# Hybrid diffusion step on one core: expert rows at fixed places, routing done tile by tile between the output products, and expert weights requested before routing

## The chip, the cores and the metric

The kernel runs on 1 core of a Trainium2 chip, in float32 throughout. The metric is the device time of one execution in microseconds (us). The kernel before takes 1537.15 us, the median of 3 runs (1534.24 to 1538.37).

## The reference

Two trunk layers over 128 context (prompt) tokens and 512 latent tokens, model width 1024. Layer 0 mixes tokens by multi-head latent attention, layer 1 by grouped-query attention; both are followed by a mixture of experts. Every sub-layer has RMS normalisation, a shift and scale, and a gate on its result; shift, scale and gate come from the conditioning vectors by one 1024 x 6144 linear map per layer (the modulation). Cut to the part around the change:

```python
for l in range(DEPTH):                                   # 2 layers
    mod_p = (silu(c_ctx) @ ada_w[l] + ada_b[l])[None]    # 6 vectors of 1024: shift, scale, gate (attention), the same (experts)
    mod_s = silu(c) @ ada_w[l] + ada_b[l]
    ...                                                  # attention; its output product is w_o (1024 x 1024)
    xp = xp + gt_a_p * mix_p;  xs = xs + gt_a_s * mix_s
    hp = modulate(rms_norm(xp, norm_ffn[l]), sh_m_p, sc_m_p);  hs = ...
    xp = xp + gt_m_p * hier_moe(hp, ...);  xs = xs + gt_m_s * hier_moe(hs, ...)

def hier_moe(h, ...):                                    # 640 tokens, 4 groups of 4 experts
    g_prob = softmax(xt @ w_group + b_group);  g_w, g_idx = top_k(g_prob, 1)
    e_in = (xt @ w_exp + b_exp)[the 4 experts of group g_idx]
    e_val, e_idx = top_k(e_in, 2);  e_w = softmax(e_val) * g_w
    out = sum over the 2 experts of e_w * (silu(xt @ w_gate) * (xt @ w_up)) @ w_down    # 1024 x 256, 256 x 1024
```

The outputs are the normalised tokens of both groups and the keys and values of the context tokens.

## The kernel before

Tokens lie in five tiles of 128 rows (tile 0 the prompt, 1 to 4 the latents). Each engine has one program, written out in order; engines hand over by semaphores. SP (SyncE) issues the weight loads in one fixed order; ScalarE's queue issues small loads and stores; POOL (GpSimd) issues the zeroing and the indexed scatters and gathers.

**Stages.** (1) Modulation products of layer 0's first columns, `ada(j)`, L1199: each takes a 1024 x 384 piece of `ada_w` (1.57 MB), on four column groups of TensorE; ScalarE copies the result out and stores it (`mod_out`, L498), and `mod_fetch` (L511) loads the pieces back for VectorE's `modulation` (L788). There are 32 such products: 6 ahead of the projection (`ADA_START`), 16 in the heads of layer 0 (two per head pair, hooks at steps 2 and 9 of ten), 10 in the heads of layer 1. (2) The projection of layer 0, tile by tile (`projection`, L1341), VectorE and ScalarE working on the result of tile t (`post_m`, L916; L684 to L694) before TensorE may start tile t + 1. (3) The heads (`heads`): eight head pairs of ten steps, each step scores, maximum, exponential, scaling, transposes and value product. (4) The mixes: `mix(l, it)`, L1238, the attention output product of one tile, 16 products of 128 x 512 (two records each). VectorE adds the result to the residual (L842) and makes the normalised, modulated tile `h` (L1107 to L1114). TensorE transposes it (`turn_h`), ScalarE copies it out, and `logits(t)` (L1430) multiplies it by the 20 router columns, two tiles behind the mixes. (5) When all five tiles have logits, `routing(l)` (L1004) picks group and experts for all tiles at once, TensorE ranks the rows of each expert (L1453 to L1455), and VectorE works out for every token and choice a row in the table `slot_rows`, for each of 25 possible tiles its expert, and how many tiles are needed. Only then POOL scatters: ten indexed DMAs of 128 rows (L461). (6) SP waits for `routed`, requests gate and up weights of the first two tiles and the down weights of the first (L367 to L371), waits for all scatters, and loads the rows of the first three tiles (L360). Expert rows are packed: an expert's rows begin at the tile behind the last of the expert before. (7) The expert loop: for each tile, rows in, transpose (L1465), gate and up (L1473), down (L1490), rows back to the table (L637). 17 tiles ran in layer 0 and 19 in layer 1. Weights lie in a ring of four slots (L284 to L293), which also serves `w_o`, `w_uq` and layer 1's q, k, v weights. (8) Gathers (L472), weighting, residual.

The table (25 x 128 rows of 1024) is zeroed by POOL from the end of layer 0's projection on (L453 to L455), 25 DMAs of 512 KB. At step 6 of the last head pair (L583 to L594) ScalarE's queue requests six broadcast rows (two of them the attention gates, `gate_a`) and the router's weights. The modulation of layer 1's first columns (`mod_fetch(1, 0)`, L615; `modulation(1, 0)`, L1117; `turn_mods(1)`, L1457) stands behind the routing of layer 0.

## Time and profile before

| | |
|---|---|
| median of 3 runs | 1537.15 us |
| profiled execution | 1533.43 us, its span 1531.6 us |
| mean granted TensorE clock | 0.905 of 2.4 GHz |
| TensorE busy | 1252.3 us (82%) |
| VectorE, ScalarE, POOL busy | 538.3, 408.0, 62.0 us |
| HBM read, written | 229.48 MB, 45.96 MB |

The page of the profile gives the span in 40 slices of 38.3 us; each digit is a busy share in tenths, and PEclk the granted clock in tenths:

```profile
PE   3487999999989609999929994999989609999980
PEclk8698999999999759999969996999989759999995
DMA  9904822333410097999982005430110087999955
```

Slices 0 to 3 are loads and the projection of layer 0, 4 to 11 its heads, 12 and 13 the mixes and routing, 14 to 19 the experts; 20 to 29 are layer 1's projection and heads, 30 to 33 mixes and routing, 33 to 38 the experts. A low PE digit with a low clock digit is a place where TensorE waits.

### The profile page before, as it was taken

The numbers are of one execution on the slowest core, as the hardware profiler recorded it, in microseconds if no ns is written. First come the engines' busy times: TensorE is split into PE (matmuls) and PEld (weight loads), VectorE is DVE, ScalarE is ACT, GpSimd is POOL, SyncE is SP. The second block draws the span as 40 slices with busy tenths as digits, with TensorE's granted clock in tenths as the row PEclk, the third lists the DMA queues.
The fourth block names the chain that finished last, engine by engine and source line by source line (L and its number), as shares of the span: only waits on it lengthen the run. The fifth ranks groups of instructions, "written<-read, shape, count | busy, mean of one in ns | idle before, by whom it ended". The sixth has DMA issues, their size and how long they took to land.

```text
span 1531.6 us, 16577 instructions
## 1 busy us (share of the span) xinstructions
PE 1252.3 (82%) x5784; PEld 687.5 (45%) x5784; DVE 538.3 (35%) x1115; ACT 408.0 (27%) x807; POOL 62.0 (4%) x70
## 2 busy tenths in 40 slices
PE   3487999999989609999929994999989609999980
PEld 0254566666645404444414542555545404444430
DVE  0231444445523311111136454566623311111116
ACT  2022344444421100111122225666621100111113
POOL 0003200000000020000020000000000020000002
PEclk8698999999999759999969996999989759999995
DMA  9904822333410097999982005430110087999955
GB/s 342 358 4 109 267 93 92 117 97 118 138 45 0 13 325 252 361 373 370 312 299 96 0 1 179 136 133 32 38 48 1 26 303 252 371 364 363 377 206 205
DMA packets 161284, 276.32 MB, mean 180 GB/s; under 512 B 12017, under 2 KB 122820, under 8 KB 160836
## 3 DMA queue, kind: packets, MB, share of 16 engines
q1 hardware_dynamic: 135440, 207.77, 39.1%
q0 software_dynamic: 9360, 34.08, 6.7%
q10 hardware_dynamic: 16420, 33.62, 6.1%
q8 instruction: 40, 0.66, 0.2%
q14 instruction: 24, 0.20, 0.0%
HBM read 229.48 MB, written 45.96 MB: 180 GB/s over the span
## 4 chain that ended last, share of the span: by engine, by line
PE 77%; DVE 7%; DMA 5%; SPq 3%; ACT 3%; issue 2%; ACTq 1%; DVEq 1%; POOL 1%; POOLq 0%
PE ps L1473 16%; PE ps L1235 10%; PE ps L1194 9%; PE ps L1253 9%; PE ps L1490 8%; PE ps L1284 6%; PE ps L1406 5%; PE ps L1373 3%; PE ps L1527 3%; PE ps L1209 2%; PE ps L1366 1%; PE ps L1383 1%; DMA arena<-slot_rows 1%; DVEq L784 1%; PE ps L1433 1%
## 5 line engine op out<-in xcount | busy, mean ns | idle before, releaser
L1194 PE MATMUL ps<-const,arena 128*128 128x128 f32 (+2 forms) x1290 | 200.1, 288 | 141.9 <-DMA arena<-slot_rows 68.6
L1194 PEld LDWEIGHTS ps<-const,arena 128*128 128x128 f32 (+2 forms) x1290 | 156.8, 147 | 233.3 <-issue 69.5
L1473 PE MATMUL ps<-arena 128*128 128x512 f32 x576 | 257.4, 600 | 4.4 <-DVE arena L1121 4.4
L869 DVE TENSOR_REDUCE hst<-ps 128x1 f32<-128x640 f32 (+1 forms) x160 | 114.5, 716 | 151.9 <-PE ps L1406 88.5
L1473 PEld LDWEIGHTS ps<-arena 128*128 128x128 f32 x576 | 108.0, 193 | 128.7 <-issue 125.2
L1235 PE MATMUL ps<-arena 128*128 128x512 f32 (+2 forms) x400 | 154.8, 547 | 9.9 <-DVE arena L840 6.6
L557 ACT ACTIVATE arena<-ps 128x640 f32<-128x640 f32 (+1 forms) x160 | 99.0, 619 | 195.8 <-PE ps L1194 177.9
L1121 DVE COPY arena<-ps 128x1024 f32<-128x1024 f32 x36 | 44.1, 1224 | 301.0 <-PE ps L1194 300.9
L1253 PE MATMUL ps<-arena 128*128 128x512 f32 x320 | 138.8, 593 | 1.8 <-issue 1.8
L1490 PE MATMUL ps<-arena 128*128 128x512 f32 x288 | 129.7, 593 | 1.9 <-DVE arena L1130 1.9
L562 ACT ACTIVATE arena<-ps,hst 128x640 f32<-128x640 f32 (+1 forms) x160 | 112.6, 704 | 17.5 <-DVE hst L869 17.5
L1235 PEld LDWEIGHTS ps<-arena 128*128 128x128 f32 x400 | 77.6, 196 | 82.8 <-issue 70.1
L1284 PE MATMUL ps<-arena 128*64 128x128 f32 x1344 | 106.6, 287 | 0.4 <-ACT arena L557 0.4
L1406 PE MATMUL ps<-arena 128*128 128x320 f32 (+1 forms) x288 | 93.3, 442 | 1.4 <-issue 1.4
L1253 PEld LDWEIGHTS ps<-arena 128*128 128x128 f32 x320 | 60.2, 190 | 74.9 <-issue 74.9
L1284 PEld LDWEIGHTS ps<-arena 128*64 128x64 f32 x1344 | 71.8, 138 | 48.0 <-issue 42.6
L627 ACT ACTIVATE arena<-ps 128x256 f32<-128x256 f32 x36 | 13.8, 384 | 295.3 <-PE ps L1473 295.3
L877 DVE TENSOR_SCALAR arena<-arena,hinv 128x640 f32<-128x640 f32 (+1 forms) x160 | 80.7, 504 | 12.8 <-issue 0.4
L1490 PEld LDWEIGHTS ps<-arena 128*128 128x128 f32 x288 | 52.1, 190 | 54.9 <-issue 52.6
L634 ACT ACTIVATE arena<-ps 128x1024 f32<-128x1024 f32 x36 | 36.8, 1023 | 140.9 <-PE ps L1490 140.9
L1209 PE MATMUL ps<-arena,cond 128*2 128x384 f32 x512 | 53.6, 541 | 19.8 <-DMA arena<-in_ada_w 13.4
L1527 PE MATMUL ps<-arena 64*128 64x320 f32 (+1 forms) x288 | 61.5, 478 | 6.6 <-ACT arena L739 4.8
(141 smaller groups left out, 874.6 us busy)
## 6 DMA issues: line engine op xcount, KB each, us to landing
arena<-in_ada_w SPq DMA_DIRECT2D x64, 768.0 KB, 6.3
arena<-in_moe_w_gate SPq DMA_DIRECT2D x36, 1024.0 KB, 7.1
arena<-in_moe_w_up SPq DMA_DIRECT2D x36, 1024.0 KB, 9.7
arena<-in_moe_w_down SPq DMA_DIRECT2D x72, 512.0 KB, 9.1
arena<-slot_rows SPq DMA_DIRECT2D x36, 512.0 KB, 10.6
slot_rows<-arena ACTq DMA_DIRECT2D x36, 512.0 KB, 7.1
slot_rows<-arena POOLq DMA_DIRECT2D x25, 512.0 KB, 12.2
arena<-mod_rows ACTq DMA_DIRECT2D x16, 512.0 KB, 6.2
```

Of the source, the lines that this page charges most:

```text
L557: act.activation(ptbuf(l, j, keys), ps[:, 4 * BANK:4 * BANK + keys], ACT.Copy).then_inc(S("pt_ready"), 1)
L562: act.activation(split(pbuf(l, s, keys), 2 if keys > P else 1), scores(s, keys), ACT.Exp, bias=hst[:, b:b + 1], accum_out=hsum[:, b:b + 1] ...
L869: nc.vector.tensor_reduce(hst[:, b:b + 1], scores(s, step(s)[3]), AX.XY, ALU.max, negate=True)\
L1194: return nc.tensor.transpose(out, in_, ident[0:rows, 0:rows])
L1209: last = mm(ada_bank(j)[ADA_Q * g:ADA_Q * g + 2, :], c[:, k], w[:, k], start=r == 0, stop=r == KD // ADA_G - 1)
L1235: last = mm(bank(2 + b, cols), hT[l](t)[:, k * P:(k + 1) * P], w[:, k], start=k == 0, stop=k == KD - 1)
L1253: last = mm(bank(mix_bank(it) + half), oT_block(l, k, it), w[:, k], start=k == 0, stop=k == KD - 1)
L1284: last = mm(oT_out(it)[VD * odd:VD * (odd + 1)], v_of(2 * m + odd, first + j), ptbuf(l, 2 * p + odd, blocks * P)[:, j * P:(j + 1) * P], st ...
L1406: last = mm(scores(s, keys)[:, c], m_qT[:, at:at + P], m_kT[:, k:k + w], start=True, stop=True)
L1473: last = mm(bank(2 + u % 2), e_xsT[:, (u % 2) * D + k * P:(u % 2) * D + (k + 1) * P], w[:, k], start=k == 0, stop=k == KD - 1)
L1490: last = mm(bank(6 + n), e_hidT[:, (u % 2) * FF + k * P:(u % 2) * FF + (k + 1) * P], w[:, k, n * BANK:(n + 1) * BANK], start=k == 0, stop= ...
L1527: last = mm(scores(s, keys)[:, c], g_qT[half, q:q + P], g_kT[half, at:at + w], start=True, stop=True)
```

## The change

- **Fixed rows.** Expert e has rows 640 e to 640 e + 639 of the table, whatever the others get; the first 16 tiles are the first 128 rows of experts 0 to 15, and only tiles beyond an expert's first are worked out (`OVER` = 9 of them). The table has 10,368 rows (a spare tile at the end) and is zeroed in 11 DMAs. Rows are read and written by an address read from `first_row`.
- **Routing tile by tile.** `pick` and `place_rows` do for one tile what `routing` did for five, two tiles behind the mixes; POOL scatters a tile's two copies when `slotted` says so. What is left of `routing` is the numbering of the overflow tiles and the weights; it stands behind the copy of the first transposed rows.
- **Router on column groups.** The router's 20 columns, padded to 32, are the stationary operand, on four column groups; ScalarE copies the 128 x 128 result out and a matmul with a selection matrix sums the groups and transposes back. The mix is cut into four parts, with router pieces between them.
- **Early weights.** Gate and up weights of experts 0 and 1 are requested before the mixes (layer 0) or in the heads (layer 1), down 0 and gate and up 2 when the mixes end. The ring starts two slots further.
- **Modulation.** Ten products move from layer 1's heads into layer 0's projection, two per tile; the other 16 of the layer 0 heads are now all of layer 1. `mod_fetch`, `mod_store` and `modulation(l, 1)` move from head pair 5 to head pair 0. `gate_a` is fetched behind the heads. Layer 1's first columns are turned behind the second mix of layer 0.

```diff
@@ SP: the loads
         def experts(l):
-            R = rounds_needed(sp, l)
-            e, e1 = expert_of(0), expert_of(1)
-            load_gu(l, 0, e)
-            load_gu(l, 1, e1)
-            load_dn(l, 0, e)
+            load_gu(l, 0, 0)
+            load_gu(l, 1, 1)
+            sp.wait_ge(S("mixed"), NTILE * (l + 1))
+            load_dn(l, 0, 0)
+            load_gu(l, 2, 2)
             sp.wait_ge(S("rows_scattered", l), 16 * 2 * NTILE)
             load_rows(l, 0, 0)
             load_rows(l, 1, 1)
+            sp.wait_ge(S("gu_done", l), 1)
+            load_dn(l, 1, 1)
             load_rows(l, 2, 0, 1)
+            load_rows(l, 3, 1, 2)
+            R = rounds_needed(sp, l)
...
         load(S("dkv_landed"), w_dkv, A["mla_w_dkv"][0], KV)
+        sp.wait_ge(S("mod_landed"), 64)
+        for j in range(ADA_START, ADA_START + 4):
+            load_ada(j)
         load(S("uk_landed"), w_uk, A["mla_w_uk"], D)
         load(S("uv_landed"), w_uv, A["mla_w_uv"], D)
-        sp.wait_ge(S("ada_made"), 4)
+        for j in range(ADA_START + 4, ADA_N - 2):
+            load_ada(j)
         load(S("uq_landed"), w_uq, A["mla_w_uq"], HEADS * P)
+        for j in range(ADA_N - 2, ADA_N):
+            load_ada(j)
         load(S("wo_landed", 0), w_wo0, A["mla_w_o"][0], BANK, 0)
-        for j in range(ADA_START, ADA_START + 2 * PAIR):
+        for j in range(ADA_N, 2 * ADA_N):
             load_ada(j)
         sp.wait_ge(S("made"), len(MAKES) * PAIR)
         load(S("wo_landed", 0), w_wo1, A["mla_w_o"][0], BANK, BANK)
+        sp.wait_ge(S("ada_made"), 2 * ADA_N)
         R = experts(0)
@@ POOL
-        for t in range(SLOT_TILES):
-            pool.dma_start(split_rows(slots[t * P:(t + 1) * P, :]), bmid(zeros, KD)).then_inc(S("table_zeroed"), 16)
+        for a in range(0, ROWS, KD * P):
+            b = min(a + KD * P, ROWS)
+            n = (b - a) // P
+            pool.dma_start(slots[a:b, :].rearrange("(p r) n -> p r n", r=n), bmid(zeros, n)).then_inc(S("table_zeroed"), 16)
         for l in range(2):
-            pool.wait_ge(S("routed", l), 1)
             for t in range(NTILE):
+                pool.wait_ge(S("slotted", l), t + 1)
                 for c in range(2):
                     pool.indirect_dma_start(
...
@@ ScalarE
         def experts(l):
+            act.wait_ge(S("pv_done"), NTILE * PAIR * (l + 1))
+            for v in range(2):
+                rows_in(gate_a[:, v * D:(v + 1) * D], l, 2, v, S("gates_a", l))
+            if l == 0:
+                mod_fetch(1, 0)
+            for t in range(NTILE + 2):
+                if 2 <= t:
+                    parts_out(t - 2)
+                if 1 <= t <= NTILE:
+                    hT_out(t - 1)
...
@@ VectorE
+        def pick(l, t):
+            lg, o, m = rt(T_LG, NR), rt(T_O, NR), rt(T_M, G5)
+            dve.wait_ge(S("logits", l), t + 1)
+            op(nc.vector.tensor_tensor(lg, bank(2, NR, P), rbias[:, l * NR:(l + 1) * NR], ALU.add)).then_inc(S("logits_in", l), 1)
+            first_max(o, lg, m, rt(T_MX, G5), rt(T_SC, NR), G5)
+            ...
+            op(nc.vector.tensor_tensor(M, m12[:, 0:NE], m12[:, NE:], ALU.add)).then_inc(S("picked", l), 1)
+            ...
+        def place_rows(l, t):
+            dve.wait_ge(S("ranked", l), t + 1)
+            op(nc.vector.tensor_tensor(tb, bank(3, NE, t * NE), const[:, C_EB:C_EB + NE], ALU.add))
+            op(nc.vector.tensor_tensor(split(t2, 2), split(m12, 2), bmid(tb, 2), ALU.mult))
+            op(nc.vector.tensor_reduce(pl, split(t2, 2), AX.X, ALU.add))
+            op(nc.vector.tensor_copy(slot_i[:, 2 * t:2 * t + 2], pl)).then_inc(S("slotted", l), 1)
...
             for t in range(NTILE):
+                if t >= 2:
+                    pick(l, t - 2)
                 residual(l, t)
+                if t >= 2:
+                    place_rows(l, t - 2)
                 row_stats(f"ffn{l}", t, t + 1, t)
                 ...
-            routing(l)
-            if l == 0:
-                modulation(1, 0)
+                if l == 0 and t == 1:
+                    modulation(1, 0)
+            pick(l, NTILE - 2)
+            place_rows(l, NTILE - 2)
+            pick(l, NTILE - 1).then_inc(S("shifted", l), 1)
+            place_rows(l, NTILE - 1)
             xsT(0, 0)
+            routing(l)
             hid(0, 0)
@@ TensorE
                 project(l, t, parts, out_sem)
+                if l == 0:
+                    for j in ada_between(t):
+                        ada(j)
...
+            for t in range(NTILE):
+                mix(l, t, 0)
+                if t >= 2:
+                    logits_part(t - 2)
+                mix(l, t, 1)
+                if t >= 2:
+                    logits(t - 2)
+                mix(l, t, 2)
+                mix(l, t, 3)
+                if t >= 2:
+                    rank(t - 2)
+                if t >= 1:
+                    turn_h(t - 1)
+                if l == 0 and t == 1:
+                    turn_mods(1)
+            logits_part(NTILE - 2)
+            logits(NTILE - 2)
+            turn_h(NTILE - 1)
+            logits_part(NTILE - 1)
+            logits(NTILE - 1)
+            rank(NTILE - 2)
+            rank(NTILE - 1)
```

`logits_part(t)` is 8 products with the router's 32 columns stationary and 128 token columns moving; `logits(t)` is the one with the selection matrix; `rank(t)` is one product for tile 0, two for tiles 1 to 3 and four for tile 4. VectorE's copy of the latents in step 4 of the last head pair of layer 0 waits for `table_zeroed`, since the zeros lie where that copy goes.

## Rows read from the trace of the kernel before

**Rows 1.** Stages by window: us, busy PE, PEld, DVE, ACT, POOL, PEclk, DMA share, GB/s.

```profile
77.00:90.00 13.00, 10.81 (x46) 7.58 (x46) 5.38 (x20) 3.00 (x11) 0.00 (x0) 1.00 0.03 11
526.00:577.00 51.00, 3.89 (x16) 3.13 (x16) 13.25 (x71) 1.51 (x2) 9.71 (x10) 0.50 0.71 254
600.00:766.00 166.00, 166.00 (x494) 80.93 (x493) 28.14 (x43) 20.73 (x29) 0.00 (x0) 1.00 1.01 356
```

**Rows 2.** The chain of waits, layer 0, mix to experts: start us, us, what.

```profile
497.69 13.73 PE ps L1253 x32
553.20 11.96 DMA slot_rows<-arena,slot_i
565.18 9.14 DMA arena<-slot_rows
577.65 8.83 PE ps L1473 x16
600.40 6.87 PE ps L1473 x16
```

**Rows 3.** The chain of waits, layer 1, the same stretch.

```profile
1187.18 13.73 PE ps L1253 x32
1266.18 9.30 PE ps L1473 x16
```

**Rows 4.** Timeline, layer 0: start us, us, engine line op out<-in [idle before <-releaser].

```profile
519.46 1.97 PE L1194 MATMUL ps<-const,arena 128*128 128x128 f32 x8 [1.68 <-DVE arena L1114]
528.83 0.17 DVE L1038 TENSOR_REDUCE arena<-arena 128x5 f32<-128x20 f32 x1 [0.28 <-issue]
531.60 0.17 DVE L1053 TENSOR_TENSOR arena<-arena 128x5 f32<-128x5 f32 x1
541.71 1.03 POOL L461 DMA_INDIRECT slot_rows<-arena,slot_i  x1 [364.15 <-DVE expert L1094]
541.87 1.01 DVE L798 TENSOR_REDUCE modt<-arena 32x128 f32<-32x512 f32 x1 [0.21 <-issue]
543.32 0.34 DVE L802 SCALAR_TENSOR_TENSOR modt<-modt,mod_vec 32x128 f32<-32x128 f32 x1
```

**Rows 5.** DMA to landing by source line: L360, then L461, then L472.

```profile
DMA to landing us min/median/max: 3.2/10.6/12.6
DMA to landing us min/median/max: 3.8/10.1/12.0
DMA to landing us min/median/max: 4.4/6.3/10.3
```

**Rows 6.** Chain after layer 0's second mix; VectorE's timeline there.

```profile
464.99 13.73 PE ps L1253 x32
469.92 1.23 DVE L1114 TENSOR_TENSOR arena<-arena 128x1024 f32<-128x1024 f32 x1
```

**Rows 7.** The chain of waits in the heads of layer 1.

```profile
1013.21 1.41 PE ps L1209 x16
1035.28 1.41 PE ps L1209 x16
1080.32 0.82 DVE hst L869
1099.58 0.82 DVE hst L869
```

**Rows 8.** Timeline at the end of those heads: ScalarE's queue, then TensorE.

```profile
1108.33 4.80 ACTq L593 DMA_DIRECT2D rw<-in_moe_w_expert  x1
1114.08 1.30 PE L1194 MATMUL ps<-const,arena 128*128 128x128 f32 x5 [6.55 <-ACT arena L557]
```

**Rows 9.** Layer 0: the chain before its projection; TensorE's timeline in it.

```profile
49.63 8.05 DMA mod_vec<-in_vec_m
90.09 9.28 PE L1235 MATMUL ps<-arena 128*128 128x384 f32 x32 [1.90 <-DVE arena L840]
```

**Rows 10.** DMA queue of POOL from 135 to 192 us: packets, MB, share.

```profile
q0 software_dynamic: 3596, 13.11, 80.9%
```

More of the change, by code:

```diff
@@ L1061, in routing @@
-            nc.vector.tensor_tensor(before[:, 0:NE], M1[:, 0:NE], M2[:, 0:NE], ALU.add)
-            for t in range(1, T5):
-                settle()
-                last = nc.vector.tensor_tensor(before[:, t * NE:(t + 1) * NE], before[:, (t - 1) * NE:t * NE],
-                                               M[:, t * NE:(t + 1) * NE], ALU.add)
-            last.then_inc(S("picked", l), 1)
-            dve.wait_ge(S("ranked", l), 1)
-            op(nc.vector.tensor_tensor(split(over, NE), blast(bank(3, NE, T5 * NE), T5), bmid(const[:, C_OV:C_OV + T5], NE), ALU.is_gt))
+            over, nt, cs, c2 = new(LAT * NE), new(NE), new(NE), new(NE)
@@ L1070, in routing @@
+            excl, av = new(NE), new(NE)
+            ge1, ge2 = new(OVER * NE), new(OVER * NE)
+            te, row, dummy = new(OVER), new(OVER), new(OVER)
+            need, rnd, den = new(ROUNDS), new(1), new(T5)
+            assert n[0] <= 1024, n[0]
+            op(nc.vector.tensor_tensor(split(over, NE), blast(bank(3, NE, T5 * NE), LAT), bmid(const[:, C_OV + 1:C_OV + T5], NE), ALU.is_gt))
             op(nc.vector.tensor_reduce(nt, split(over, NE), AX.X, ALU.add))
@@ L1092, in routing @@
+            op(nc.vector.tensor_tensor(dummy, dummy, const[:, C_DUM:C_DUM + OVER], ALU.mult))
+            nc.vector.tensor_scalar(te, te, float(NE - 1), None, ALU.min)
+            op(nc.vector.tensor_tensor(row, row, dummy, ALU.add))
+            nc.vector.tensor_copy(first_row[:, 0:NE], const[:, C_EB:C_EB + NE])
+            nc.vector.tensor_copy(first_row[:, NE:], row)
+            nc.vector.tensor_copy(expert[:, 0:NE], const[:, C_TI:C_TI + NE])
             nc.vector.tensor_copy(rounds[:, 0:1], rnd)
@@ L1247, in mix @@
                 pe.wait_ge(S("pt_ready"), (l + 1) * STEPS)
-            if it >= 2:
+            if it >= 2 and part == 0:
                 pe.wait_ge(S("mix_out"), l * NTILE + it - 1)
-            for half in range(2):
-                w = split(halves[half], KD)
-                for k in range(KD):
-                    last = mm(bank(mix_bank(it) + half), oT_block(l, k, it), w[:, k], start=k == 0, stop=k == KD - 1)
-            last.then_inc(S("mixed"), 1)
+            half, ks = part // 2, range(KD // 2 * (part % 2), KD // 2 * (part % 2 + 1))
+            w = split((w_wo0, w_wo1)[half], KD)
+            for k in ks:
+                last = mm(bank(mix_bank(it) + half), oT_block(l, k, it), w[:, k], start=k == 0, stop=k == KD - 1)
+            if part == 3:
+                last.then_inc(S("mixed"), 1)
         def spare_free(l, m, r):
@@ L1428, in turn_h @@
                 last.then_inc(S("h_turned", l), 1)
-            def logits(t):
-                pe.wait_ge(S("hT_out", l), t + 1)
-                for k in range(KD):
-                    last = mm(bank(2, NR, t * 32), e_hT[:, (t % 2) * D + k * P:(t % 2) * D + (k + 1) * P], rw[:, k * NR:(k + 1) * NR],
-                              start=k == 0, stop=k == KD - 1)
-                last.then_inc(S("logits", l), 1)
-            mix(l, 0)
-            mix(l, 1)
-            turn_h(0)
-            pe.wait_ge(S("router_landed", l), 32)
@@ L1441, in experts, with logits_part @@
-            for t in range(2, NTILE):
-                mix(l, t)
-                logits(t - 2)
-                turn_h(t - 1)
+            def logits_part(t):
+                pe.wait_ge(S("hT_out", l), t + 1)
+                if t:
+                    pe.wait_ge(S("logits_in", l), t)
+                for r in range(KD // ADA_G):
+                    for g in range(ADA_G):
+                        k = ADA_G * r + g
+                        last = mm(bank(2, P)[RWC * g:RWC * (g + 1)], rw[:, k * RWC:(k + 1) * RWC],
+                                  e_hT[:, (t % 2) * D + k * P:(t % 2) * D + (k + 1) * P], start=r == 0, stop=r == KD // ADA_G - 1)
+                last.then_inc(S("logits_part", l), 1)
@@ new lines, in logits, with rank @@
+            def logits(t):
+                pe.wait_ge(S("parts_out", l), t + 1)
+                mm(bank(2, NR, P), e_LT, const[:, C_SEL:C_SEL + NR], start=True, stop=True).then_inc(S("logits", l), 1)
+            def rank(t):
+                pe.wait_ge(S("picked", l), t + 1)
+                M, before = e_r[:, R_M + t * NE:R_M + (t + 1) * NE], e_r[:, R_BEF + t * NE:R_BEF + (t + 1) * NE]
+                last = mm(bank(3, NE, t * NE), tri, M, start=True, stop=t == 0)
+                if t:
+                    last = mm(bank(3, NE, t * NE), ones, before, start=False, stop=True)
+                if t == NTILE - 1:
+                    mm(bank(3, NE, NTILE * NE), ones, before, start=True, stop=False)
+                    last = mm(bank(3, NE, NTILE * NE), ones, M, start=False, stop=True)
+                last.then_inc(S("ranked", l), 1)
```

263 lines of the change are left out of this document (134 added, 129 removed).

## The prediction

> **What bounds the kernel now.** I read the page's slices first: TensorE is busy 82% of the span, and there are two holes of about 50 us, one in each layer, between the attention output product (the "mixes", L1253) and the expert loop (L1473). Then I read the stages by window. In the hole TensorE works 3.89 of 51 us at clock 0.50, the low level of 1.2 GHz; in the expert loop it works 166.00 of 166 us at full clock, although DMA is full as well (share 1.01) [rows 1]. So the expert loop is TensorE's, and the time to be won lies in the hole. The chain of waits shows what is in it [rows 2, 3]: the fifth mix ends at 497.69 + 13.73 = 511.42, the first expert product starts at 577.65, which is 66.2 us; in layer 1 it is 1266.18 − 1200.91 = 65.3 us. In order: last normalised tile and its transposes, router logits, one routing calculation for all five tiles on VectorE (small operations that start every (531.60 − 528.83) / 11 = 0.25 us), ten scatters issued 1.28 us apart ((553.20 − 541.71) / 9), 11.96 us until the last has landed, 9.14 us until rows are back, transpose, copy [rows 2, 4]. Both landings run beside 5.2 MB of expert weights that are requested only after routing. In the heads TensorE sets the pace too: a head pair of layer 1 with two modulation products takes 1035.28 − 1013.21 = 22.07 us, one without takes 1099.58 − 1080.32 = 19.26 us, and the difference is twice the 1.41 us of one product [rows 7].
>
> **The hole after the change.** T is the end of the fifth mix. Picks and placings of tiles 0 to 2 now lie beside the mixes (5.8 us of small operations in a period of (497.69 − 464.99) / 2 = 16.35 us [rows 2, 6], of which VectorE uses about 6), and weights of experts 0 to 2 are in before they are needed. What stays behind T is serial:
> 1. The last tile's transposes start at T + 8.0 (519.46 − 511.42), as before, and take 2.0; copy 1.1. T + 11.1 [rows 4].
> 2. Router part: 16 records. The nearest are 16 records of 384 columns, also on four column groups, in 1.41 us at full clock [rows 7], 2.8 at the low one; with 128 columns I take 2.0 (0.7 to 3.6). Copy and selection matmul 0.8. T + 13.9.
> 3. Rank and place tile 3, which wait behind these on TensorE: 0.5 + 1.1. T + 15.5.
> 4. Pick tile 4: about 19 small operations at 0.25, 4.8; ranking it ends 0.3 later; place 1.0. T + 21.6.
> 5. Two scatters instead of ten: the second starts at T + 22.9. It lands in 3.8 to 12.0 us; a gather of the same size with little beside it has a median of 6.3 [rows 5], which I take. T + 29.2.
> 6. Rows back: 3.2 to 12.6 us [rows 5]; with only one other load beside it I take 4.0. Transposes 2.0, copy 1.2, hand-overs 0.3. T + 36.7.
>
> That saves 66.2 − 36.7 = 29.5 and 65.3 − 36.7 = 28.6: **−58.1 us**. The calculation for the overflow tiles (some 30 operations, 7 us) now comes after the first row copy; it lies beside the first expert product, which takes 8.83 us [rows 2], and would cost its full 7 us without it. The indexed scatters take no more DMA than before.
>
> By the Trainium skill (DMA: Bandwidth & Descriptors, "Anatomy of one DMA — SWDGE (gpsimd) path") such a DMA costs about 2.0 us plus its bytes over 436,000 per us, 3.2 us for these 512 KB. The quickest scatter here took 3.8 and the median 10.1 [rows 5], so the trace shows the queue beside it, not the formula. By the formula step 5 would be 3.1 us shorter in each layer and the sum 6 us lower.
>
> **Layer 1's modulation columns.** In layer 0 TensorE is to transpose them after the second mix, and they come from VectorE behind that mix's residual and normalisation. The normalised tile is done at 469.92 + 1.23 = 471.15 [rows 6]; the three operations take 543.66 − 541.87 = 1.8 [rows 4], the transpose 0.3: 473.3. Today the third mix starts at 464.99 [rows 6], so TensorE stands for 8.3 us, and every later mix waits behind it. Today this work sits in the hole and costs nothing. After such a stop the clock is low; 16 records took 8.83 instead of 6.87 us [rows 2], so 2.0 more. **+10.3 us** (0 if it were hidden, 13 at most).
>
> **Router pieces between the mixes.** A selection matmul and a rank are new in each tile and three tiles' logits lie before T, not two: some 2 us a layer (−1 to +4), **+4 us**.
>
> **Ten modulation products moved from the heads of layer 1 to layer 0's projection.** Out: five head pairs by 22.07 − 19.26 = 2.81, **−14.1 us** [rows 7]; TensorE is the limit there, so it is paid back in full. In: two by 1.41 a tile; TensorE waits 1.90 us for VectorE ahead of a projection [rows 9], so 0.9 of 2.8 remains, four times; behind the last tile ScalarE copies and stores two results ahead of the copies that TensorE waits for, about 3.3. +6.9. Their 15.7 MB have an almost idle DMA (0.03) [rows 1], but two slots, and 5.2 MB of other weights on SP's queue between them: 21 MB at the 356 GB/s of the expert loop [rows 1] are 59 us of the 76 from 60 to 136. SP now also holds all that back until the first modulation input has landed, which took 8.05 us behind those loads [rows 9] and should take about 3.2, the quickest load of another kind [rows 5]: −4.9. Net **+2 us** (−6 to +20).
>
> **ScalarE's DMA requests.** Near the end of each layer's heads it issues six broadcasts and the router's weights; the last one holds it 4.80 us and TensorE stands 6.55 us [rows 8]. The six are 3.1 MB, 8.8 us at 356 GB/s, so I read the stop as a queue that must drain. Two of the six move behind the heads (under the first mix, 13.7 us, against the 6.2 us to landing that the page gives): 1 MB less, up to 2.9; I take 2.5 twice, **−5 us** (0 to −6). The row-address read added to each load and store falls where SP and ScalarE wait for TensorE: 0.
>
> **Zeroing.** The table grows from 3200 to 10,368 rows, 13.1 to 42.5 MB. 13.11 MB took 80.9% of 57 us [rows 10], 46 us of full DMA, so 42.5 MB take 149; the heads of layer 0 add 25 MB of modulation weights, about 70 us. That fits into the 275 us from 136 to the copy that waits for it (step 4 of the last head pair, about 411): 0.
>
> **Number of expert tiles.** L1473's 576 records are 36 tiles. Counting the reference's choices on its inputs gives 38 to 118 and once 128 rows per expert in layer 0 and 28 to 200 in layer 1: none is empty, 16 and 19 tiles are needed, and both ways of numbering run 17 and 19. 0.
>
> **Sum**: −58.1 + 10.3 + 4 − 14.1 + 2 − 5 = −60.9 us. The profiled execution took 1533.43 us (span 1531.6), so 1472.5; the median of the runs shown, 1537.15, is 3.7 higher, which gives **1476 us**.
>
> **Rivals.** (A) The holes shrink less: the last scatter and the first rows land at their loaded 12.0 and 12.6 us, because 1 MB of gate rows and later requests fall on them. +14.3 a layer: 1505. The rows' medians of 10 speak for it, against it that the weights have landed by then. (B) Layer 0's projection is starved of modulation weights: a pair 4 us late in each of four tiles, +16: 1492. For it: only two slots and the loads put between; against: 17 us of slack in the bytes. (C) Slower than before: the zeroing is late and VectorE's copy in the last head pair waits for it, holding all of attention. It decides once the queue moves less than 42.5 MB in 275 us, 155 GB/s (it had 285 while busy); since 61 us are won elsewhere, the whole is slower only if it ends after 411 + 61 = 472, under 126 GB/s. At 110 GB/s it ends at 522: +111, 1587. (D) The numbering does not do what it says and runs two tiles more in each layer, 22.8 us each: 1522.
>
> A rule that would bring (A) and (C) nearer is in the Trainium skill (SBUF — State Buffer, the warning on "DVE blocks DMA"): GpSimd can't write descriptors while VectorE is in certain fast modes. The scatters of the hole went out 1.28 us apart [rows 4], but most of them beside an idle VectorE, so no row here tests it; by the rule each scatter between the mixes and each zeroing request could be held by up to one VectorE operation.
>
> **How the numbers follow.** Forecast 0.70, with its own range 1462 to 1492; A 0.12, B 0.12, C 0.04, D 0.02. The range of 1460 to 1506 takes in A and B. This kernel's runs tell about 0.3% (5 us) from no change. Faster 0.95, within 0.3% 0.01, slower 0.04.
>
> **What would show it.** Holes of 35 to 40 us from the fifth mix to the first expert product, with the last scatter landing near T + 29; a TensorE stop of about 8 us after the second mix of layer 0 and none in layer 1; head pairs of layer 1 all near 19.3 us; POOL's zeroing queue empty before 370. I am wrong if a hole is over 45 us, if TensorE waits for modulation weights in layer 0's projection by more than 5 us, or if the head pairs of layer 1 stay above 21.

## The result and the profile after

| | before | after |
|---|---|---|
| median, beside each other on one chip | 1535.70 us | 1459.39 us (1457.22 to 1460.94, 4 runs) |
| profiled execution, its span | 1533.43, 1531.6 us | 1459.84, 1457.6 us |
| TensorE busy, mean granted clock | 1252.3 us, 0.905 | 1244.3 us, 0.93 |
| HBM written | 45.96 MB | 75.32 MB |

The change makes the kernel faster: ratio 0.9497 (95% interval 0.9478 to 0.9517). The forecast was 1476 us with a range from 1460 to 1506; the time lies 0.6 us below the range, and 17 us below the forecast. Like with like: I worked out 1472.5 us for the profiled execution, and it took 1459.84. So 12.7 us of the miss are in the terms of the sum; the other 4 come from adding 3.7 us for the step from the profiled execution to the median, where the changed kernel's median lies 0.45 below its profiled execution. The slices of the page, 36.4 us each:

```profile
PE   3598899999997958999965997799999859999970
...
DMA  9699999422272064999965002400020348999955
```

The two holes are narrower (slices 14 and 32; in the kernel before, layer 0's hole is slices 13 and 14 and its experts begin in slice 15). The DMA is full in slices 2 to 6 as well: first with the ten modulation products' weights, and from 135.4 us on (slice 3) with the larger zeroing, which writes most of the 63.44 MB of POOL's queue. By window (columns as in [rows 1]):

```profile
77.00:90.00 13.00, 13.00 (x78) 7.77 (x77) 5.24 (x18) 4.46 (x13) 0.00 (x0) 1.00 1.04 389
...
200.00:260.00 60.00, 60.00 (x410) 38.00 (x404) 30.13 (x72) 28.23 (x65) 0.00 (x0) 1.00 1.03 413
260.00:300.00 40.00, 40.00 (x274) 25.91 (x276) 19.55 (x44) 16.47 (x37) 0.00 (x0) 1.00 0.30 100
```

Layer 0's projection now runs with a full DMA and a busy TensorE, where the DMA share was 0.03 [rows 1]; the zeroing beside the heads is over near 260 us.

The chain of waits from layer 0's second mix to the experts, which answers to [rows 2] and, for layer 0, [rows 4] (start us, us, what):

```profile
470.31 0.31 PE ps L1257
470.62 6.50 PE ps L1313 x8
477.12 0.57 PE ps L1500 x16
...
489.46 3.44 PE ps L1313 x8
...
513.23 6.97 PE ps L1313 x16
...
527.27 1.98 PE ps L1257 x8
...
530.35 1.12 PE ps L1500 x16
...
534.10 0.17 DVE slot_i L1103
...
540.66 0.18 DVE slot_i L1103
...
542.36 6.00 DMA slot_rows<-arena,slot_i
548.38 3.15 DMA arena<-slot_rows
...
554.86 8.81 PE ps L1556 x16
...
577.60 6.87 PE ps L1556 x16
```

And layer 1's hole, which answers to [rows 3]:

```profile
1151.30 6.97 PE ps L1313 x16
...
1180.42 4.42 DMA slot_rows<-arena,slot_i
1184.86 3.31 DMA arena<-slot_rows
...
1191.49 8.78 PE ps L1556 x14
```

With T the end of the fifth mix (520.20 and 1158.27), the holes are 34.7 and 33.2 us. The stop for layer 1's modulation columns is in layer 0 alone: TensorE is done with the second mix at 461.56 and with the transposes behind it at 462.4, and the third mix starts at 470.62. Between mixes a router piece (L1500) takes 0.57 us; in the kernel before, 16 records of one took 1.70 us:

```profile
478.73 1.70 PE ps L1433 x16
```

Sorted by stage, in us, from the ends of the stages in the two chains:

| stage | change | forecast |
|---|---|---|
| start to the end of layer 0's projection | −1.0 | +2 |
| what follows it, and the heads of layer 0 | −1.5 (+3.8 and −5.3) | −2.5 |
| mixes of layer 0, of layer 1 | +11.35, +0.1 | +10.3, and +4 for both |
| hole of layer 0, of layer 1 | −31.6, −32.1 | −29.5, −28.6 |
| experts and projection of layer 1, tail | +2.8 | 0 |
| heads of layer 1 | −22.1 (−14.2 and −7.9) | −14.1 − 2.5 |
| sum | −74.0 | −60.9 |

The +3.8 is what is left when the −5.3 of ScalarE's requests (read further down) is taken out of the −1.5. The −14.2 is left in the same way.

### The profile page after: what moved, and what is told of

It is laid out like the page before. It is cut to its first block, busy times and chain, and to the rows that moved or that the text cites. A ratio compares the mean times of both kernels' runs of the same rounds, so it can differ in the third digit from the quotient of the medians.

```text
span 1457.6 us, 17210 instructions
## 1 busy us (share of the span) xinstructions
PE 1244.3 (85%) x5836; PEld 674.5 (46%) x5836; DVE 566.0 (39%) x1291; ACT 412.3 (28%) x818; POOL 53.8 (4%) x57
## 3 DMA queue, kind: packets, MB, share of 16 engines
q0 software_dynamic: 16304, 63.44, 11.1%
HBM read 229.51 MB, written 75.32 MB: 209 GB/s over the span
## 4 chain that ended last, share of the span: by engine, by line
PE 79%; DVE 7%; DMA 5%; ACT 3%; SPq 2%; issue 1%; ACTq 1%; DVEq 1%; POOL 0%; POOLq 0%
PE ps L1556 17%; PE ps L1257 10%; PE ps L1313 10%; PE ps L1298 10%; PE ps L1573 9%; PE ps L1344 6%; PE ps L1469 6%; PE ps L1436 3%; PE ps L1611 3%; PE ps L1272 2%; DMA arena<-in_ada_w 2%; PE ps L1429 2%; PE ps L1446 1%; DVEq L825 1%; DVE hst L910 1%
## 5 line engine op out<-in xcount | busy, mean ns | idle before, releaser
L1257 PE MATMUL ps<-const,arena 128*128 128x128 f32 (+2 forms) x1290 | 199.7, 288 | 90.8 <-DVE arena L863 29.5
L1556 PE MATMUL ps<-arena 128*128 128x512 f32 x576 | 257.7, 601 | 4.4 <-DVE arena L1183 4.4
L1556 PEld LDWEIGHTS ps<-arena 128*128 128x128 f32 x576 | 108.2, 193 | 128.8 <-issue 125.4
L1313 PE MATMUL ps<-arena 128*128 128x512 f32 x320 | 144.7, 606 | 1.7 <-issue 1.7
L1573 PE MATMUL ps<-arena 128*128 128x512 f32 x288 | 129.7, 593 | 2.0 <-ACT arena L672 1.1
L593 ACT ACTIVATE arena<-ps,hst 128x640 f32<-128x640 f32 (+1 forms) x160 | 112.7, 705 | 17.3 <-DVE hst L910 17.1
L665 ACT ACTIVATE arena<-ps 128x256 f32<-128x256 f32 x36 | 13.8, 385 | 214.0 <-PE ps L1556 214.0
```

What stands on the lines that cost most here:

```text
L593: act.activation(split(pbuf(l, s, keys), 2 if keys > P else 1), scores(s, keys), ACT.Exp, bias=hst[:, b:b + 1], accum_out=hsum[:, b:b + 1] ...
L1257: return nc.tensor.transpose(out, in_, ident[0:rows, 0:rows])
L1313: last = mm(bank(mix_bank(it) + half), oT_block(l, k, it), w[:, k], start=k == 0, stop=k == KD - 1)
L1556: last = mm(bank(2 + u % 2), e_xsT[:, (u % 2) * D + k * P:(u % 2) * D + (k + 1) * P], w[:, k], start=k == 0, stop=k == KD - 1)
L1573: last = mm(bank(6 + n), e_hidT[:, (u % 2) * FF + k * P:(u % 2) * FF + (k + 1) * P], w[:, k, n * BANK:(n + 1) * BANK], start=k == 0, stop= ...
```

## The experiments

Each was timed beside the kernel before. Ratios are to that; differences between variants are of medians and, where a trace is shown, of stages. The changed kernel was timed again only beside e9, e10 and e11 (as e12: 1460.38 us), so a difference of 1 to 3 us between it and e6 or e7 is at the limit of what can be told.

**Early weights and tile-wise scatter, undone one at a time and together.** e1 requests the first weights only once routing is done, and those of expert 2 only behind the first tile's gate and up products:

```
+            sp.wait_ge(S("slotted", l), NTILE)
             load_gu(l, 0, 0)
             load_gu(l, 1, 1)
-            sp.wait_ge(S("mixed"), NTILE * (l + 1))
             load_dn(l, 0, 0)
-            load_gu(l, 2, 2)
             sp.wait_ge(S("rows_scattered", l), 16 * 2 * NTILE)
...
             sp.wait_ge(S("gu_done", l), 1)
+            load_gu(l, 2, 2)
```

> The kernel after (1459.4 us, profiled holes of 34.7 and 33.2 us from the fifth mix to the first expert product), with the first expert weights requested only when all five tiles have their rows. Theory 1 (the DMA queue beside the last scatter is what the early request takes away): the last scatter lands in about 10 instead of 6.0 and 4.4 us and the first rows in about 9 instead of 3.2 us, so each hole grows by 8 to 12 us and the time goes to 1475 to 1483. Rival (the holes are set by the operations on VectorE and TensorE alone, and the weights could as well come late): holes within 2 us of those of the kernel after, time 1457 to 1463.

Measured: 1498.10 us (1494.74 to 1499.22), ratio 0.9731 (0.9708 to 0.9754), 39 us over the changed kernel, more than either theory gave. The chain of layer 0 shows why:

```profile
542.19 0.37 SPq L360
...
543.22 4.94 SPq L360
548.20 5.61 SPq L360
...
557.29 9.15 DMA arena<-slot_rows
...
569.77 9.98 PE ps L1556 x16
...
582.91 9.13 DMA arena<-slot_rows
...
598.51 6.87 PE ps L1556 x16
```

There are two effects in the hole. Six weight requests stand ahead of the first rows on SP's queue and hold it until 557.29, although SP finds the scatters landed when it gets there; and the rows then take 9.15 us beside 5.2 MB. The hole is 569.77 − 521.48 = 48.3 us (47.0 in layer 1), 13.6 and 13.8 more than with the change. The rest, some 11 us, lies behind the first product of each layer, and the early weights as such do not account for it. In e1 SP requests the gate and up weights of expert 2 once that product is done, then the second tile's down weights, and only then the third tile's rows, for which TensorE waits (582.91). From the first product to the third tile's it is 28.7 us (598.51 − 569.77) and 28.4 in layer 1. In the changed kernel it is 22.74 (577.60 − 554.86) and 23.6, and in the kernel before, whose weights are late too, 22.75 (600.40 − 577.65, [rows 2]): there SP requests the third tile's rows right behind the first two, ahead of that tile's weights. So of e1's 39 us, 27.4 in the two holes are what early weights are worth, and the other 11 come from e1's own order of requests.

e2 lets POOL scatter nothing before all five tiles are placed:

```
             for t in range(NTILE):
-                pool.wait_ge(S("slotted", l), t + 1)
+                pool.wait_ge(S("slotted", l), NTILE)
```

> The kernel after, with POOL starting its ten scatters only when all five tiles have their rows. Theory 1 (issue on POOL is serial, 1.28 us each, and eight of ten now lie behind the last tile): each hole grows by 8 x 1.28 = 10.2 us, and up to 3 more for landing behind the others, time 1480 to 1486. Rival (ten scatters queue up in the DMA engines at once, so the last lands at its loaded 10 us or more): 15 us or more a hole, time above 1489.

Measured: 1481.51 us (1478.68 to 1483.71), ratio 0.9635 (0.9612 to 0.9658), 22 us over the changed kernel. The holes are 562.74 − 518.20 = 44.5 and 43.8 us, 9.9 and 10.6 more: eight more scatters at 1.25 to 1.28 us on POOL, 10.2. The last one lands in 5.03 us, where two alone had 6.00 and 4.42, so ten scatters one behind the other do not slow each other here:

```profile
551.11 5.03 DMA slot_rows<-arena,slot_i
```

e3 has both edits.

> The kernel after with both undone: weights requested and all scatters started only when all five tiles have their rows; what is left of the change in the hole is the tile by tile routing. If the two effects share the DMA engines (5.2 MB of weights and 5.2 MB of scatters, 10.5 MB at about 370 GB/s are 28 us), the holes grow by more than the sum of the two alone or near it, 18 to 24 us each, time 1495 to 1508. If the ten issues (12.8 us) hide the weights, the holes grow by 10 to 14 us only, as with the scatters alone, time 1480 to 1488.

Measured: 1517.39 us (1515.51 to 1520.86), ratio 0.9864 (0.9838 to 0.9890). 58 us over, against 39 + 22 = 61 for the two apart, and above both ranges that I gave. The hole is 580.59 − 522.42 = 58.2 us in layer 0 and 56.8 in layer 1, 23.5 and 23.6 more than with the change: inside the 18 to 24 of the theory that they share the engines, and not the 10 to 14 of an overlap. Another 9.7 us are again the third tile's rows. In SP's queue (chain of layer 0) one weight request is held for 15.68 us while the ten scatters run:

```profile
548.69 15.68 SPq L360
```

In e1 the same request took 5.61 us. In layer 1 it took 4.32 us, and a request of down weights behind it 13.29.

Now the holes can be divided. They are 8.1 and 8.4 us shorter in e3 than in the kernel before: that is what is left of the change there, the routing tile by tile and the earlier transposes. Early weights add 27.4 (e1), scatters tile by tile 20.5 (e2). That makes 64.4 us, against the 63.6 measured.

**Which part of the early weights is the queue?** e9 is e1 with the first two row loads taken out of SP's queue and put on ScalarE's:

```
+            act.wait_ge(S("rows_scattered", l), 16 * 2 * NTILE)
+            for u in range(2):
+                act.dma_start(e_xs[:, u * D:(u + 1) * D], slots[u * CAP:u * CAP + P, :]).then_inc(S(f"xs_landed{u}", l), 16)
```

> The kernel of the late weights (1498.1 us, holes of 48.3 us in layer 0), with the rows of the first two tiles requested from ScalarE's queue as soon as the scatters have landed, instead of from SP's queue behind the weights. Theory 1 (the weights hold SP's queue, so that the row loads are requested about 10 us after the scatters have landed): the holes shrink by 5 to 10 us, time 1478 to 1488. Rival (the DMA engines are the limit and rows requested earlier only share them): holes within 2 us, 1495 to 1500.

Measured: 1487.47 us (1486.35 to 1490.13), ratio 0.9672 (0.9655 to 0.9688), 10.6 less than e1. In the chain the rows are requested when the last scatter has landed:

```profile
544.76 9.37 DMA slot_rows<-arena,slot_i
554.15 6.33 DMA arena<-slot_rows
...
563.81 8.95 PE ps L1557 x16
...
575.95 9.21 DMA arena<-slot_rows
```

The hole is 563.81 − 522.59 = 41.2 us. Of e1's 13.6 us, 7.1 were SP's queue; 6.5 are left, and they are the engines: the scatter lands in 9.37 instead of 6.00 and the rows in 6.33 instead of 3.15 us. The wait for the third tile stays (9.21 us). In layer 1 the hole is 40.9 us, 6.1 less than in e1. So in the hole the early weights work in both ways, about half each.

**Layer 1's modulation columns after the last tile.** e4 moves the modulation operations behind place_rows of the last tile (and the transpose behind TensorE's last ranking, into bank 4):

```
-                if l == 0 and t == 1:
-                    modulation(1, 0)
...
             place_rows(l, NTILE - 1)
+            if l == 0:
+                modulation(1, 0)
```

> The kernel after, with layer 1's modulation columns made and turned behind the placing of the last tile (in the time that the last scatter needs) instead of behind layer 0's second mix. Theory 1: the stop of 8.2 us after that mix and the 3.1 us of low clock behind it go, and nothing comes back, since VectorE and TensorE wait for the scatter there: 11.3 us less, about 1448, mixes of layer 0 in 75.1 us as in layer 1. Rival: TensorE is early at the next wait or the work moves into the hole: 5 us less or nothing, above 1454.

Measured: 1450.02 us (1449.41 to 1450.65), ratio 0.9427 (0.9408 to 0.9446): 9.4 us less, its span 10.4 less than the changed kernel's. The window over the mixes of layer 0 has no stop left (columns as in [rows 1]):

```profile
460.00:509.00 49.00, 49.00 (x189) 23.84 (x188) 27.26 (x87) 7.96 (x15) 4.57 (x4) 1.00 0.11 43
```

The mixes take 75.1 us instead of 86.4, and the hole stays at 543.70 − 508.65 = 35.1. The rival is out: the hole grew by 0.4 us at most, so the work did not move into it. The term of +10.3 us was a real price, and one not necessary.

**ScalarE's requests, alone.** e5 is the kernel before with the gate rows' two requests behind the heads:

```
                 for v in range(2):
-                    rows_in(gate_a[:, v * D:(v + 1) * D], l, 2, v, S("gates_a", l))
-                for v in range(2):
...
+            for v in range(2):
+                rows_in(gate_a[:, v * D:(v + 1) * D], l, 2, v, S("gates_a", l))
             for t in range(NTILE):
```

> The kernel before (1535.7 us), with one thing changed: the two broadcast loads of the attention gates are requested behind the heads, so ScalarE's queue takes four broadcasts and the router's weights near the end of the heads instead of six. Theory 1 (the queue holds only so many requests, and the sixth and the last must wait for earlier ones to drain, with a low clock behind the stop): 13 us less in both layers together (5.3 and 7.9 by the traces), time 1521 to 1525. Rival, the term as I forecast it (the stop shrinks by the transfer time of the two rows): 5 us less, 1529 to 1532.

Measured: 1524.85 us (1523.78 to 1526.22) beside 1537.09, ratio 0.9918 (0.9901 to 0.9934), 12.2 us less for one moved pair of requests in each layer, as the first theory had it. The stretch is read from the first of these requests to the first mix. In the kernel before, layer 0 and layer 1:

```profile
414.50 0.34 ACTq L536
...
436.41 27.70 PE ps L1253 x64
...
1104.17 0.34 ACTq L536
...
1125.91 27.70 PE ps L1253 x64
```

That is 21.9 and 21.7 us. In the changed kernel it is 16.6 and 13.9, so −5.3 and −7.9:

```profile
417.26 0.34 ACTq L567
...
433.84 27.72 PE ps L1313 x64
...
1069.30 0.34 ACTq L567
...
1083.17 27.70 PE ps L1313 x64
```

In e5 the chain at the end of layer 1's heads, to be read beside [rows 8], is:

```profile
1104.15 1.05 ACTq L591
...
1106.15 0.74 PE ps L1194 x5
...
1115.51 4.53 PE ps L1253 x10
```

From the first of these requests to the first mix it is 1115.51 − 1101.55 = 14.0 us; before, 21.7. Three things make the 7.8: the two requests themselves no longer stand on ScalarE (0.74 + 0.73 and their gaps, 1.5); the router weights' request holds it for 1.05 instead of 4.80 us (3.75); and what follows runs quicker (2.5), since five transposes behind the stop took 1.30 us [rows 8] and take 0.74 now. The granted clock is 0.50 in the 6 us behind the stop of the kernel before (1113 to 1119) and 1.00 in e5 (1105 to 1111). While the router weights' request holds ScalarE, the DMA is full (share 0.99 from 1108 to 1113). Layer 0 gives 1.5 + 1.7 + 2.0 = 5.2. The changed kernel's last request in layer 1 takes 1.10 us, so it is this part of it that does it.

**The other four requests, one head apart.** e6 issues them at operations 3 to 6 of the last head pair, the router's at 7:

```
-            if (m, r) == (7, 6):
+            if m == 7 and 3 <= r <= 6:
...
+                v, n = divmod(r - 3, 2)
+                rows_in(e_row[:, (2 * v + n) * D:(2 * v + n + 1) * D], l, (4, 3)[n], v, S("rows_e", l))
+            if (m, r) == (7, 7):
```

> The kernel after, with the four broadcasts of the last head pair requested one per step (steps 3 to 6) and the router's weights at step 7. Theory 1 (what is left of ScalarE's stop is the requests in a row): the stops of about 3 us in layer 0 and 2 us in layer 1 shrink, 3 to 5 us less, 1454 to 1457. Rival (each request costs ScalarE its 0.4 us wherever it stands and the rest is hidden): no difference beyond 1 us.

Measured: 1458.57 us (1457.66 to 1459.40), ratio 0.9486 (0.9470 to 0.9501). No difference that can be told from the changed kernel; what was to be had there was had with the first two. In its trace the router weights' request in layer 0 is down to 0.60 us, from 2.19, and the span is 2.2 us less.

**The modulation inputs out of the zeroing.** The four requests of mod_fetch in head pair 0 stand beside the zeroing of POOL's queue in the changed kernel. Its chain there:

```profile
177.92 1.55 ACTq L556
...
181.05 1.56 ACTq L556
```

e7 moves them, and what follows on them, to head pair 5:

```
-            if (m, r) == (0, 3):
+            if (m, r) == (5, 3):
                 mod_fetch(l, 1)
```

> The kernel after, with the fetch, the sum and the store of each layer's other modulation rows back in head pair 5, where the zeroing is over, instead of head pair 0. Theory 1 (in head pair 0 the four requests of ScalarE and its store wait behind the zeroing of the table, and TensorE with them): the heads of layer 0 are 3.8 us shorter, time about 1455.5. Rival (the 3.8 us come from modulation weights landing late or from the start of the heads): no difference.

Measured: 1456.72 us (1456.06 to 1457.04), ratio 0.9470 (0.9454 to 0.9486); its span is 2.8 us less. The traces say more than the times: the same four requests take 0.32 to 0.45 us each in head pair 5, and no request of ScalarE is in e7's chain in head pair 0. From the first head product to the second modulation product of the heads it is 27.7 us in e7 (168.23 to 195.94), 27.7 in the kernel before (169.22 to 196.93) and 32.2 in the changed kernel (167.54 to 199.71). So the stop was 4.5 us, and all of it went. The engines move modulation weights there as well (a share of 1.01 from 134 to 200); which of the two holds the requests this run doesn't tell apart. The intervals of the two ratios overlap, so how much of it the time keeps is only about what can be told.

**The zeroing made three times as large.** e8 zeroes two unused tables of the same size as well (127.4 MB in all) and waits for all of it:

```
+        for e in range(2):
+            for a in range(0, ROWS, KD * P):
...
-        pool.wait_ge(S("table_zeroed"), 16 * ZEROINGS)
+        pool.wait_ge(S("table_zeroed"), 48 * ZEROINGS)
```

> The kernel after, zeroing two more tables of the same size that nobody uses (127 instead of 42.5 MB), with VectorE's copy in the last head pair waiting for all of it. By rival C's mechanism as I priced it: the engines moved 394 to 413 GB/s while zeroing and modulation weights ran together, so 127 + 27 MB need about 380 us, from 135 to 515, and the copy at about 415 waits 100 us: 1555 to 1565. If zeroing instead slows the other loads first (modulation weights of the heads), TensorE waits in the heads before that copy and the total grows by more than the wait alone, over 1575.

Measured: 1559.84 us (1559.21 and 1560.47), ratio 1.0142 (1.0122 to 1.0163), slower than before: 100 us over the changed kernel, in one piece of the chain. VectorE's copy (L907) starts behind it, at 514.37:

```profile
414.50 99.85 another core or an unknown queue
```

The profile calls the releaser unknown; it is the zeroing, for nothing else differs. The copy waits at 414.50 and goes on at 514.35, so 127.4 MB and what ran beside them ended 379 us after they began at 135.4. The mechanism of rival (C) is real; at 42.5 MB it has 150 us to spare.

**One load from in front of the modulation weights.** e10 requests w_uq (3.1 MB) behind layer 0's last modulation weights:

```
-        load(S("uq_landed"), w_uq, A["mla_w_uq"], HEADS * P)
         for j in range(ADA_N - 2, ADA_N):
             load_ada(j)
+        load(S("uq_landed"), w_uq, A["mla_w_uq"], HEADS * P)
```

> The kernel after, with the 3.1 MB of the query weights requested behind the last two modulation weights of layer 0's projection. If the wait of 2.07 us of TensorE for the last modulation weights is on the path: 2 us less, about 1457.5. If ScalarE's copies behind the last tile set the end of the projection anyway: within 1 us of 1459.4.

Measured: 1458.21 us (1456.94 to 1458.92) beside 1460.38 for the changed kernel in the same set; ratios 0.9478 (0.9462 to 0.9494) and 0.9489. The times alone leave this within what can be told. The traces decide it: the one wait that the edit could remove is the 2.07 us of the changed kernel,

```profile
124.33 2.36 PE L1272 MATMUL ps<-arena,cond 128*2 128x384 f32 x16 [2.07 <-DMA arena<-in_ada_w]
```

and in e10 it is gone: both products run in one piece (2.76 us from 120.50), and the first head product starts at 164.40, against 167.54 in the changed kernel and 167.28 in e12. The wait was on the path.

**A version that beats both.** e11 joins the edits of e4, e6 and e7; e12 is the changed kernel once more, in the same set.

> The kernel after with three edits at once: layer 1's modulation columns behind the last placing (10 us less alone), the other modulation rows' fetch in head pair 5 (2.7 us less alone), ScalarE's requests one per step (1 us less alone). If they add: 1445 to 1447. If two of them hide the same wait: 1449 or more.

> The kernel after, unchanged, beside the others on one chip, as the reference for differences of a few us: 1457 to 1461.

Measured: e11 1442.34 us (1441.57 to 1443.05), ratio 0.9372 (0.9357 to 0.9388); e12 1460.38 us (1457.70 to 1461.72), ratio 0.9489 (0.9473 to 0.9505). 18 us less than the change alone, and 3 us below what I had expected if the three add. In spans the three parts gave 10.4 + 2.8 + 2.2 = 15.4 of the 17.1 us; 1.7 I can't place. The first mix starts at 429.39 instead of 433.84, the mixes take 75.1 instead of 86.4 us, the holes stay at 35.2 and 33.5.

## Why the prediction was right, and where it was wrong

The direction, the place of the gain and all four rivals came out as weighed: no hole over 45 us (A), projection of layer 0 not starved (B), zeroing over long before its reader (C), 576 products in L1556, so 36 tiles (D). The mechanism of (A) is real: beside late weights the last scatter took 9.37 us and the first rows 9.15 (e9, e1). It stayed away because the weights had landed. The terms do not fit as well as that: one was mis-sized by 8.2 us and three by 3 to 6 us (the holes, the router pieces, the start), 20.7 us in the same direction, and 7.7 us of cost that I had at nothing or too low stand against them. That the time came within 0.6 us of the range owes something to luck.

**The step that failed is "ScalarE's DMA requests".** "I read the stop as a queue that must drain … 1 MB less, up to 2.9; I take 2.5 twice, −5 us (0 to −6)". Measured: −5.3 and −7.9 = −13.2 in the changed kernel, and −13.0 in e5, which has nothing else of the change. That the stop goes when two requests go is right; the price was not. I counted only the hold of the last request, and by its bytes. Shown in layer 1 are 1.5 for the two requests' own time on ScalarE, 3.75 for the hold, and 2.5 for the TensorE that follows at the low clock. The first and the third stood in rows I had: a request's own duration and the five transposes of 1.30 us [rows 8]. The bound of −6 left them out. With −5 here and all else as measured the time would be 1467.6 us, inside the range. But 0.6 us is little, and any one of the other misses of 3 us or more decides it too.

**The holes**: −63.6 against −58.1. Step by step for layer 0 (forecast, measured, from T):

| step | forecast | measured |
|---|---|---|
| 1 copy of the last normalised tile | 11.1 | 10.1 |
| 2, 3 router, rank and place tile 3 | 15.5 | 14.1 |
| 4 tile 4 placed | 21.6 | 20.6 |
| 5 second scatter out, landed | 22.9, 29.2 | 22.2, 28.2 |
| 6 first expert product | 36.7 | 34.7 |

The order of steps is as written. Overestimates of 0.6 to 1.5 us add up: the router part on four column groups took 1.12 us at the low clock, where I took 2.0 (the transposes, though, began at T + 7.1, which also gains 0.9), and the rows 3.15 where I took 4.0. In layer 1 the scatter landed in 4.42 us, where I took 6.3 and layer 0 had 6.00, which makes 33.2. The Trainium skill (DMA: Bandwidth & Descriptors, "Anatomy of one DMA — SWDGE (gpsimd) path") would have 3.2 us for it. The trace has 6.00 and 4.42 at the place that matters, and 3.3 us as the quickest of its 20 scatters, so here the formula is near the quickest scatter and not the price in the hole.

**Early weights.** I said only that they "are in before they are needed". e1 shows that this is worth 27.4 us in the two holes, more than the tile-wise scatter (20.5), and e9 that about half of it is an order of requests in one queue. I had it inside steps 5 and 6 without a price of its own.

**Layer 1's modulation columns**: forecast +10.3, measured +11.35 in the stage, of which the stop is 8.2 (8.3 forecast) and the slower part behind it 3.1 (2.0 forecast: 6.50 for eight records against 3.44, with a granted clock of 0.50 from 470.6 to 474). e4 gets 10.4 of it back.

**Router pieces**: forecast +4, measured about 0.1 in layer 1. I counted what is new and not what gets cheaper. New in the mixes are one logits piece more, 0.13 us for each selection (L1506) and 0.13 for the first tile's rank, 0.35 for the second's (L1511, L1513), and some 0.3 a tile for the mix in pieces (3.44 + 3.63 + 6.96 against 13.73). But 16 records of logits take 0.57 instead of 1.70 us: three pieces now cost 1.7 where two cost 3.4.

**Ten modulation products**: out −14.1 forecast, −14.2 measured. The head pairs of layer 1 now follow each other in 19.3 us (VectorE's first reduction of each, in the chain, at 1045.45 and 1064.71).

In: +2 forecast, −1.0 measured. The modulation input landed in 1.83 us, where I took 3.2 and it had been 8.05 [rows 9]:

```profile
49.49 1.83 DMA mod_vec<-in_vec_m
```

With it the first projection starts 6.4 us earlier (4.9 forecast). The ten products then cost 5.3 (6.9 forecast), 2.07 of them the wait that e10 removes.

**What I did not see**: the requests of mod_fetch in head pair 0 take 1.12 to 1.56 us each beside the zeroing, where such requests took 0.36 and 0.44 us at 48 us of the chain, before the zeroing. They stop TensorE for 4.5 us, which is the +3.8 of the table with 0.65 us won just before. I had moved POOL's queue in my sum only as a transfer with a deadline, not as company for ScalarE's requests. e7 gets 2.8 of the span back. Another +2.8 us stand in the experts, the projection of layer 1 and the tail, where I had put nothing. 0.6 of them are the last tile's store behind layer 0's experts, whose address is now read first, and 1.2 the first tile of layer 1's projection (22.55 us against 21.33, at a lower granted clock, 0.91 against 0.96). The rest I did not trace.

**Zeroing**: forecast 0, measured 0 at its deadline. My 149 us of full DMA for 42.5 MB plus 70 us for the weights would end at 354. It ended near 260, since the DMA moved 394 to 413 GB/s here, where I had put 285 for POOL's queue [rows 10]. By the Trainium skill (SBUF — State Buffer, the warning on "DVE blocks DMA") scatters between the mixes might have been held by VectorE. The trace has both cases. Tile 3's pair goes out while VectorE picks tile 4, in small operations, and the second of tile 1's pair starts 0.5 us into VectorE's operation L1171, which runs 1.28 us over a whole tile (POOL's timeline):

```profile
509.14 1.60 POOL L492 DMA_INDIRECT slot_rows<-arena,slot_i  x1 [0.30 <-issue]
...
534.55 0.95 POOL L492 DMA_INDIRECT slot_rows<-arena,slot_i  x1 [7.82 <-DVE slot_i L1103]
```

Beside small operations a scatter takes 0.95 us and they start 1.26 us apart, as those beside an idle VectorE did (1.28). The one beside L1171 takes 1.60. So do all five of the 20 scatters that start some 0.5 us into that operation (1.59 to 1.60 us, in both layers). The first two scatters of layer 0, one begun before it and one 0.13 us ahead of its end, took 1.02 and 1.00. That fits the rule in direction, at 0.65 us each; whether L1171 runs in such a mode no run shows. It cost nothing here, since no such scatter is in the chain.

## What to carry to other kernels

When a DMA request blocks the engine that issues it, count its cost in three parts: the requests' own time on that engine, the hold, and the low clock of TensorE after the stop; a pair of requests moved 9 to 14 us later in each layer was worth 13 us here, over a sixth of the total gain. When weights and a late, small input share one issuing queue, put the weights so early that they are in before that input is wanted, or put the input on another queue; look at when the request was issued, not only at how long the transfer took. A small calculation that is off the critical path where it is goes onto it if TensorE must take a part in it between two long products: put it where TensorE already waits.

## What the runs showed of the hardware

- What a request costs the engine that issues it depends on what was requested before it, and not in proportion: the same request took 4.80 us behind six broadcasts of 512 KB and 1.05 to 1.10 us behind four (in layer 0 4.07, and 2.41 in e5, 2.19 in the changed kernel, 0.60 with the four spread over steps in e6). What fills up, descriptors or bytes, no run here tells apart.
- The same is seen on SP: the first two requests of 1 MB took 0.37 and 0.58 us, the next two 4.94 and 5.61 (e1), and the fourth 15.68 beside ten scatters (e3, layer 0).
- Requests of ScalarE that took 0.32 to 0.45 us elsewhere took 1.12 to 1.56 us while POOL's queue held the zeroing (e7 against the changed kernel).
- An indexed scatter takes POOL 0.95 us, and 1.60 when it starts 0.5 us into VectorE's 1.28 us operation L1171 (five of 20).
- The DMA moved 413 GB/s over 60 us with writes of zeros and weight loads together, against 356 in the expert loop [rows 1], and up to 420 GB/s in a slice of the page of e8.
- Of ten scatters of 512 KB issued 1.25 us apart (e2) the last lands no later after its issue than that of two: 5.03 us, against 6.00 and 4.42. Beside weight loads it takes 9.37 (e9), and took 11.96 in the kernel before [rows 2].
